# Two-layer decoder step: expert weight blocks in a ring of seven buffers, and the index-key loads moved behind the last expert's blocks

## The reference, cut to what matters

```python
y = jnp.zeros((m, d), jnp.float32)
for e in range(N_EXPERTS):
    hid = jax.nn.silu(x2 @ w_gate[e]) * (x2 @ w_up[e])
    y = y + combine[:, e:e + 1] * (hid @ w_down[e]).astype(jnp.float32)
```

```python
dots = jnp.einsum('nqhe,nke->nqhk', qi_blk, k_idx) * idx_scale
score = jnp.einsum('nqhk,nqh->nqk', jax.nn.relu(dots), wi_blk)
```

## Time and profile before

| | us |
|---|---|
| median of 3 runs (lowest, highest) | 1475.85 (1475.16, 1477.64) |
| the profiled execution: its own time | 1472.07 |
| its span | 1470.3 |
| TensorE busy in the span | 1311.3 (89%) |
| VectorE, ScalarE, GpSimd busy | 577.5, 306.4, 184.2 |
| bytes moved by DMA | 341.06 MB, mean 232 GB/s |

### The profile page before, as it was taken

One profiled execution on the slowest core, in us unless ns is written; L12 is line 12 of the kernel. 1 busy time (PEld: TensorE's weight loads), 2 busy tenths in 40 slices (PEclk: granted clock), 3 DMA queues, 4 the chain that ended last, 5 costly groups with the idle time before them and its releaser, 6 DMA issues. The chain is left out here.

```text
span 1470.3 us, 27309 instructions
## 1 busy us (share of the span) xinstructions
PE 1311.3 (89%) x10905; PEld 734.8 (50%) x10906; DVE 577.5 (39%) x1433; ACT 306.4 (21%) x785; POOL 184.2 (13%) x469
## 2 busy tenths in 40 slices
PE   7999999999599999886799998889995999998990
PEld 3444455544365556553644444555543655555550
DVE  2059944443523111011648995565216131111115
ACT  2121144421100000001313115555402000000002
POOL 1010082010100000002102661000101000000002
PEclk9999999999699999998799998999997899999995
DMA  9451489934587999999201133331514589999966
GB/s 283 166 157 59 147 289 324 347 130 129 183 332 277 394 394 399 404 413 357 63 1 58 33 115 116 115 116 59 229 72 172 198 322 360 394 387 400 406 273 204
DMA packets 87597, 341.06 MB, mean 232 GB/s; under 512 B 25843, under 2 KB 33107, under 8 KB 73506
## 3 DMA queue, kind: packets, MB, share of 16 engines
q1 hardware_dynamic: 67466, 289.49, 52.5%
q0 software_dynamic: 10656, 37.56, 7.4%
q10 hardware_dynamic: 9344, 12.20, 2.4%
HBM read 309.09 MB, written 30.47 MB: 231 GB/s over the span
## 5 line engine op out<-in xcount | busy, mean ns | idle before, releaser
L1255 PE MATMUL banks<-arena 128*32 128x128 f32 (+1 forms) x4736 | 355.0, 332 | 26.9 <-DMA arena<-in_wstream 13.0
L1255 PEld LDWEIGHTS banks<-arena 128*32 128x32 f32 (+1 forms) x4736 | 237.5, 125 | 143.9 <-issue 47.4
L1283 PE MATMUL banks<-arena 128*64 128x512 f32 (+1 forms) x1184 | 173.0, 492 | 1.1 <-ACT arena L1751 1.1
L930 PE MATMUL banks<-arena 128*128 128x512 f32 x320 | 143.9, 604 | 1.4 <-DMA arena<-in_wstream 1.4
L1857 DVE TENSOR_TENSOR arena<-arena,banks 128x256 f32<-128x256 f32 (+5 forms) x84 | 38.5, 459 | 269.4 <-PE banks L1255 175.9
L2228 DVE COPY arena<-banks 128x256 f32<-128x256 f32 (+1 forms) x56 | 21.4, 382 | 294.0 <-PE banks L1268 287.7
L1857 DVE TENSOR_TENSOR arena<-banks,arena 128x512 f32<-128x512 f32 (+5 forms) x159 | 70.6, 474 | 131.6 <-ACT arena L1673 86.0
L1158 PE MATMUL banks<-arena 128*128 128x512 f32 x256 | 113.9, 602 | 3.6 <-ACT arena L1791 2.3
L958 PE MATMUL banks<-arena 128*128 128x512 f32 x256 | 116.5, 600 | 0.0
L1751 ACT ACTIVATE arena<-banks 128x512 f32<-128x512 f32 (+1 forms) x56 | 29.6, 529 | 366.7 <-PE banks L1283 366.7
L1283 PEld LDWEIGHTS banks<-arena 128*64 128x64 f32 (+1 forms) x1184 | 58.6, 123 | 84.4 <-issue 70.0
(11 more groups left out here) (292 smaller groups left out, 1421.3 us busy)
## 6 DMA issues: line engine op xcount, KB each, us to landing
arena<-in_wstream SPq DMA_DIRECT2D x109, 2048.0 KB, 13.4
arena<-in_fox_kt SPq DMA_DIRECT2D x64, 256.0 KB, 4.5
arena<-in_fox_v SPq DMA_DIRECT2D x64, 256.0 KB, 4.2
arena<-in_dsa_page SPq DMA_DIRECT2D x64, 256.0 KB, 4.1
expert_rows<-arena ACTq DMA_DIRECT2D x76, 128.0 KB, 9.0
expert_rows<-arena POOLq DMA_DIRECT2D x1, 6656.0 KB, 20.3
hn_scratch<-arena POOLq DMA_DIRECT2D x8, 512.0 KB, 3.0
expert_rows<-arena ACTq DMA_DIRECT2D x68, 32.0 KB, 8.3
```

Of the source, the lines that this page charges most:

```text
L930: last = mm(bank(job % 4), xt[:, c, c0:c1], w[:, c, :], start=(c == 0), stop=(c == DC - 1))
L1255: last = mm(bank(b, 0, 4 * n, n * j, n * j + n), x[:, c, :], w[:, c, 4 * n * j:4 * n * j + 4 * n], start=(c == 0), stop=(c == DC - 1))
L1283: last = mm(bank(3, 0, 8 * n, n * q, n * q + n), ht2[g % 2][:, 128 * i + n * j:128 * i + n * j + n], w[:, c, 8 * n * q:8 * n * q + 8 * n], ...
```

## The change

The buffers of the expert weights become one ring of seven for each layer: the six of before and `QT` 0 to 4096 as the seventh. Block n of the layer (n = 3 s + i) goes into buffer n % 7 and waits for the use of block n-7. The first six blocks are loaded as before; block 6 (expert 2's gate) is the first in the seventh buffer and waits for nothing but `ranked`.

Index keys also live in `QT` 0 to 4096, so their 64 loads leave the early part of SP's list. They now stand behind all expert blocks of layer 0, after a wait until expert 13's down products are done (the last user of the seventh buffer), and ahead of the three blocks of layer 1's input projection, of `last_rows(0)` and of all that follows.

Semaphores are merged: `lf_dve` and `lf_act` become `lf`, and `ln_var`, `ln_root` and `ln_done` become `ln`, with counts that stand for the same events.

```diff
+SLOTS = 7
...
+              "weights": tuple(16 * len(range(i, 3 * NE, SLOTS)) for i in range(SLOTS)),
...
-    slots = [[[ring[2], ring[0], ring[1]], over_w], [[ring[1], ring[2], ring[0]], over_w]]
+    slots = [[ring[i] for i in first] + over_w + [at("QT", 0, 4096)] for first in ((2, 0, 1), (1, 2, 0))]
...
+    def slot_of_block(l, s, i):
+
+        return slots[l][(3 * s + i) % SLOTS]
+
+    def block_landed(l, s, i):
+
+        n = 3 * s + i
+        return f"weights{l}_{n % SLOTS}", 16 * (n // SLOTS + 1)
+
+    def block_used(l, s, i):
+
+        before, j = divmod(3 * s + i - SLOTS, 3)
+        name = ("gate_mm", "up_mm", "down_mm")[j] + str(l)
+        return name, upto(name, ENDS[before])
...
         def experts(l):
             b = first_block(l, "moe")
             if l == 0:
-                index_keys(0, 12)
-                sp.wait_ge(S("ln_done"), 1)
+                sp.wait_ge(S("ln"), 3)
                 first_weights(0, 1, 0)
-                index_keys(12, 24)
             sp.wait_ge(S(f"out_mm{l}"), upto(f"out_mm{l}", 5))
             first_weights(l, 0, 1)
-            if l == 0:
-                index_keys(24, 50)
             sp.wait_ge(S(f"out_mm{l}"), upto(f"out_mm{l}", 10))
             first_weights(l, 0, 2)
-            if l == 0:
-                index_keys(50, 58)
             sp.wait_ge(S(f"route_t{l}"), upto(f"route_t{l}", 3))
             first_weights(l, 1, 2)
-            if l == 0:
-                index_keys(58, NS * NPG)
             sp.wait_ge(S(f"ranked{l}"), upto(f"ranked{l}", 1))
             for s in range(2, NE):
                 k = sp.value_load(block_i[0:1, s:s + 1], min_val=0, max_val=3 * NE - 3)
-                for i, name in enumerate((f"gate_mm{l}", f"up_mm{l}", f"down_mm{l}")):
-                    sp.wait_ge(S(name), upto(name, ENDS[s - 2]))
+                for i in range(3):
+                    if 3 * s + i >= SLOTS:
+                        name, count = block_used(l, s, i)
+                        sp.wait_ge(S(name), count)
                     sp.wait_ge(S("x_in_0"), 16)
                     weights(l, s, i, a["wstream"][bass.ds(k + (b + i), 1)].rearrange("a p w -> (a p) w"))
...
         experts(0)
+        sp.wait_ge(S("down_mm0"), upto("down_mm0", ENDS[13]))
+        index_keys(0, NS * NPG)
         for b, name in ((1, "gate_mm0"), (2, "up_mm0"), (3, "down_mm0")):
             k = first_block(1, "in") + b
             sp.wait_ge(S(name), upto(name, ENDS[14]))
```

More of the change, by code:

```diff
@@ L120 @@
     (64, "vnew"),
-    (128, "xg weights"),
+    (128, "xg"),
 )
@@ L527, in weights @@
         def weights(l, s, i, src):
-            sp.dma_start(slots[l][s % 2][i], src).then_inc(S(f"weights{l}_{3 * (s % 2) + i}"), 16)
+            sp.dma_start(slot_of_block(l, s, i), src).then_inc(S(block_landed(l, s, i)[0]), 16)
         def first_weights(l, s, i):
@@ L1261, in landed @@
             def landed(s, i):
-                pe.wait_ge(S(f"weights{l}_{3 * (s % 2) + i}"),
-                           upto(f"weights{l}_{3 * (s % 2) + i}", 16 * (s // 2 + 1)))
+                name, count = block_landed(l, s, i)
+                pe.wait_ge(S(name), upto(name, count))
             def turn_hid(g):
@@ L1278, in down @@
                     pe.wait_ge(S(f"y_ev{l}"), upto(f"y_ev{l}", g))
-                w = g3(slots[l][s % 2][2], 4)
+                w = g3(slot_of_block(l, s, 2), 4)
                 for c in range(4):
@@ L1295, in experts @@
                     pe.wait_ge(S(f"silu{l}"), upto(f"silu{l}", g))
-                part_features(0, g3(slots[l][s % 2][0], DC), x, n).then_inc(S(f"gate_mm{l}"), 1)
+                part_features(0, g3(slot_of_block(l, s, 0), DC), x, n).then_inc(S(f"gate_mm{l}"), 1)
                 if g > 0:
@@ L1304, in experts @@
                     pe.wait_ge(S(f"ht_ev{l}"), upto(f"ht_ev{l}", g - 1))
-                part_features(1 + g % 2, g3(slots[l][s % 2][1], DC), x, n).then_inc(S(f"up_mm{l}"), 1)
+                part_features(1 + g % 2, g3(slot_of_block(l, s, 1), DC), x, n).then_inc(S(f"up_mm{l}"), 1)
                 if g == ENDS[s] - 1 and s + 1 < NE:
@@ L1384, in beside_even @@
                 if t == 0:
-                    pe.wait_ge(S("lf_dve"), 1)
+                    pe.wait_ge(S("lf"), 1)
                 pe.wait_ge(S("u_ready"), t + 1)
@@ L1617, in project_even @@
                 if job == 10:
[L1618 to L1621, removed]
+                    act.wait_ge(S("lf"), 1)
+                    af(lf_tmp[0], lf_tmp[0], ACT.Exp).then_inc(S("lf"), 1)
+                    act.wait_ge(S("lf"), 3)
+                    af(lf_tmp[0], lf_tmp[0], ACT.Ln).then_inc(S("lf"), 1)
                 if 12 <= job < 22:
@@ L1786, in _ @@
         af(tick[0], tick[0], ACT.Sqrt)
-        act.wait_ge(S("ln_var"), 1)
-        af(lnv, lnv, ACT.Sqrt).then_inc(S("ln_root"), 1)
-        act.wait_ge(S("ln_done"), 1)
+        act.wait_ge(S("ln"), 1)
+        af(lnv, lnv, ACT.Sqrt).then_inc(S("ln"), 1)
+        act.wait_ge(S("ln"), 3)
         for c in range(4):
@@ L2331, in _ @@
         v.scalar_tensor_tensor(out=lf_tmp[0], in0=lf_tmp[1], scalar=-1.0, in1=lf_tmp[1], op0=ALU.mult, op1=ALU.min)\
-            .then_inc(S("lf_dve"), 1)
+            .then_inc(S("lf"), 1)
         step(v.tensor_scalar(lf_tmp[2], lf_tmp[1], 0.0, None, ALU.min))
@@ L2343, in new_logf @@
         def new_logf():
-            dve.wait_ge(S("lf_act"), 1)
-            v.tensor_scalar(lf_tmp[0], lf_tmp[0], 1.0, None, ALU.add).then_inc(S("lf_dve"), 1)
+            dve.wait_ge(S("lf"), 2)
+            v.tensor_scalar(lf_tmp[0], lf_tmp[0], 1.0, None, ALU.add).then_inc(S("lf"), 1)
         def split_logf():
-            dve.wait_ge(S("lf_act"), 2)
+            dve.wait_ge(S("lf"), 4)
             tt(lft, x3[2], x3[0], ALU.subtract).then_inc(S("logf"), 1)
@@ L2418, in layer_norm @@
             v.tensor_scalar(lnv[:, 0:SEQ], bank(7), 1e-5, None, ALU.add)
-            v.tensor_scalar(lnv[:, SEQ:TOK], bank(6, 0, 64), 1e-5, None, ALU.add).then_inc(S("ln_var"), 1)
-            dve.wait_ge(S("ln_root"), 1)
+            v.tensor_scalar(lnv[:, SEQ:TOK], bank(6, 0, 64), 1e-5, None, ALU.add).then_inc(S("ln"), 1)
+            dve.wait_ge(S("ln"), 2)
             step(v.reciprocal(lnv, lnv))
             tt(xt[:, 0:4, 0:SEQ], conv_p, bc_mid(lnv[:, 0:SEQ], 4), ALU.mult)
-            tt(xt[:, 0:4, SEQ:TOK], conv_s, bc_mid(lnv[:, SEQ:TOK], 4), ALU.mult).then_inc(S("ln_done"), 1)
+            tt(xt[:, 0:4, SEQ:TOK], conv_s, bc_mid(lnv[:, SEQ:TOK], 4), ALU.mult).then_inc(S("ln"), 1)
         attend(0, 4, lambda t: causal[:, 384 - 128 * t:512])
```

## The result

The changed kernel takes 1504.59 us, the median of 4 runs (1502.66 to 1509.0), against 1475.51 us before (4 runs, 1475.14 to 1477.64): a ratio of 1.0198 (95% interval 1.017 to 1.0227), so +25 to +33 us, about +29. The forecast was 1502, +26.2.

What follows compares the result with a forecast made beforehand. It took block landing to bound the experts' second part and SP's chain the seam behind layer 0: +32.1 us for the later gather, -5.9 in layer 1, +26.2 on 1475.85, 1502 us; 8-in-10 range 1489 to 1513.

Steps and rivals of the forecast that it cites:

- The bound and the seventh buffer: Both layers' experts: later blocks set the pace; a seventh buffer gains one block's landing, 5.9 us in each layer.
- SP's time for the keys: Behind layer 0's last expert blocks: SP needs 47.7 us to issue 64 keys, plus 2 us if full queues hold it up.
- rival A: At the late keys: SP is held up to the far bound of 13.4 us, 11.4 us more, 1513 us; chance 0.15.
- The queue in front of the store: Behind the keys: the last rows' store waits for three projection blocks, 6.3 MB; third lands at 719.4, gather starts near 720.5.
- Rival B: Behind the keys: the rows store overtakes the blocks, gathers sharing engines cost up to 10.6 us; 1488 to 1499 us; chance 0.10.
- The sum at the seam: Between layer 0's experts and the combine: keys, hold-up and queue together start the gather 32.1 us later, near 720.5.
- Nothing takes the delay back: After layer 0's gather: all that follows is a chain from it, so the 32.1 us delay stays.
- The rule on small transfers: Key loads of 32 KB: overhead is SP's 0.7 us each; the coalescing rule speaks against placing them on the chain.
- The early part: Before and early in layer 0's experts: taking the key loads out is worth nothing, as TensorE is busy from 400 us.
- C: Expert stages: the seventh buffer gives nothing, since the engines are full anyway; +38 us, 1514 us; chance 0.05.
- D: Expert stages: the seventh buffer takes away all weight waits, 11.5 us more gained, 1487 us; chance 0.06.
- E: Behind layer 0's experts: key issue hides behind the last two experts, leaving only both gains, -11.8, 1464 us; chance 0.03.

Runs made afterwards that it cites:

- kernel 8: Against the kernel before: seven buffers, with projection blocks, rows store and tail weights first, then all 64 keys in one piece; 1469.58 us, ratio 0.9957.
- Kernel 3: Also rows_before_blocks: the changed kernel with the last rows' store between the keys and the three projection blocks; 1501.16 us, ratio 1.0158 to the kernel before.
- rows_by_act: The changed kernel with the last rows' store issued by ScalarE, whose queue is empty, instead of SP; 1484.09 us, ratio 1.0062 to the kernel before.
- kernel 6: Against the kernel before: seven buffers in both layers, the 64 keys spread over SP's rests in three pieces; 1468.28 us, ratio 0.9928; again 1466.94 us, 0.9935.
- kernel 7: The spread key order of kernel 6 with six buffers instead of seven; 1475.42 us, ratio 0.9986 to the kernel before.
- kernels 5: Against the kernel before: seventh buffer in layer 1 alone, layer 0 with six and its keys early; 1473.38 us, ratio 0.9961.

## Why the prediction was right, point by point

**The bound and the seventh buffer.** Right in kind, and in size over many profiles. I forecast one block in each layer, 5.9 us. The means of the table differ by 5.1 us in layer 0 and 6.4 us in layer 1; by time, the seventh buffer in layer 1 alone gave 5.8 us. TensorE's waits for blocks fall from a mean of 12.1 to 7.5 us in layer 0 and from 12.5 to 7.3 in layer 1; in the 15 stages with seven buffers 5 to 9 us of them stay, as they should when blocks land at the pace of the engines. The lead itself shows in layer 1: the last expert block landed 278.1 us behind the start of the stage before (issued at 1408.7, landed 13.4 us later), and 271.2 us in the changed kernel (1432.1, 25.8 us).

The first profile of the changed kernel alone would have misled: its layer 0 shows 289.03 us, a gain of 1.3, and its last block landed 275.2 us behind the start (issued at 643.1, landed 29.1 us later) against 275.3 before. In that one stage the lead was lost before the end. Its timeline of PE (start, us, what, idle before):

```profile
397.04 11.90 PE L1268 MATMUL banks<-arena 128*64 128x256 f32 x128 [1.11 <-DVE arena L1870]
...
645.34 5.31 PE L1268 MATMUL banks<-arena 128*64 128x256 f32 x32 [3.61 <-issue]
...
684.14 1.93 PE L1296 MATMUL banks<-arena 128*32 128x256 f32 x32 [0.53 <-ACT arena L1764]
```

Its first 128 products ran 11.90 us, against 10.71 in the profile before; the granted clock of the stage's first 12 us was 0.75 of full speed here and 0.85 there. The 32 products behind the wait of 3.61 us took 5.31 us in place of 3.67, with a granted clock of 0.72 over the 6 us from 645.34 on. These are means of stretches that ran in part at the lower of the two clock levels, 1.2 and not 2.4 GHz. Why the blocks landed late in that execution is not shown. The other six layer-0 stages with seven buffers lie between 284.3 and 287.1, so I take it for scatter.

**SP's time for the keys.** Forecast 47.7 us, and 2 us for a hold-up. Measured 50.0 in the changed kernel, 49.4 with six buffers, 47.7 in kernel 8. The sum 49.7 was right, in part by luck. The forecast put the hold-up down to full queues. A single issue took up to 1.54 us against a median of 0.469, but only one of the long ones (1.25 us, at 663) stands where expert blocks were still under way and keys took 4.5 us and more to land. Those of 1.54, 0.99 and 0.96 us stand at 679, 688 and 692, where keys landed in 3.4 us or less, and the row of kernel 8 has one of 1.58. So what makes them long stays open; nothing came near the 13.4 us of rival A. The forecast also passed over the slowest of the three rows of keys in the same view of the kernel before:

```profile
292.91 9.34 SPq L547 DMA_DIRECT2D arena<-in_kidx_t  x12
```

That is 0.78 us each, which makes 49.8 us for 64 without any second term.

**The queue in front of the store.** Forecast: 19.8 us from the first block's issue to the gather, 18.7 of them until the third block is down. Measured: 708.80 to 728.42, 19.6 us, with the third block down at 726.9, 18.1 us behind the first issue. Kernel 3 shows the cause: with the store ahead of the blocks, 3.0 us. The order on each ring that the Trainium skill states ("DMA: Bandwidth & Descriptors", queues, rings and completion order) agrees with this trace: the stores landed at about 727.0 us, behind the third block's 726.9. Its warning that completion is not first in, first out across a queue didn't show in this place. Rival B was also priced too low: the gathers then share the engines with the blocks, as said, but this costs 14.8 us and not up to 10.6.

**The sum at the seam.** Forecast: gather 41.8 us behind the experts' end (720.5 less 678.7). Measured: 42.4 and 42.7, and 42.0 with six buffers. The delay of the gather, forecast as 32.1 us, was 40.0 in the first profile and 37.3 in the second. In the first it stood at 728.42 and not 720.5: 2.8 us of that is the late start of the stage, 4.5 its small gain in layer 0, 0.6 the seam. In the second it stood at 725.75: 2.9 us are the late start, 1.4 what the gain in layer 0 fell short, 0.9 the seam. So the seam was right to 1 us, and what is left over is what differs from one execution to the next; the close total (+26.2 against +29 and +26) rests on medians in which that evens out.

**Nothing takes the delay back.** Right. From the gather to layer 1's first expert product it is 458.3 and 457.6 us in the two profiles of the changed kernel, 455.6 before, and in seven others 455.4 to 460.0. The two left are rows_by_act (473.7, with its added wait of 17.1 us) and rows_before_blocks (470.9, with its slow gathers).

**The rule on small transfers** (the Trainium skill, "DMA: Bandwidth & Descriptors", rules for kernel authors: coalesce, under 64 KB one pays mostly overhead). The keys' price was SP's 0.78 us each on the chain. But kernels 6 and 8 keep all 64 small loads, and kernel 6 loses nothing by them, kernel 8 some 3 to 4 us: here the place decided. What fewer and larger loads would have cost in the old place no run shows.

**The early part.** Costed at nothing, and kernel 7 agrees: with the keys gone from there, six buffers are no faster than before within its interval (-4.9 to +0.7 us). The start of layer 0's experts says the same: 394.2 us by the mean of the three profiles with all or half of the keys early, 394.9 by that of the nine without.

**The rivals.** A fell with the keys' row, B with kernel 3, C with kernels 5 and 7 (the same order with and without the seventh buffer: -10.7 and -2.1 us), D with the 5 to 9 us of waits that stay. E was held impossible in this order, and was: it takes another order, that of kernel 6, in which SP's time is spread between waits. There the forecast of -11.8 us for two bare gains is met by -10.7 and -9.6.

**Two slips.** The DMA digit is 9 in slices 13 to 18 and 33 to 37 of the earlier trace rows, where the forecast says 13 to 17 and 32 to 38; and 698.5 + 2 makes 700.5, not 700.7. Nothing else hangs on either.

## What to carry to other kernels

Loads that cost nothing in bytes can cost their issuer's time: count the issues by the nearest row of that queue, and ask what stands behind them in the same list. Where a stage runs at the pace of a transfer that never rests, one more buffer was worth about one block's landing time, once, and not the sum of the waits. To free one held-up instruction shows only who is late next; put the short stores and the first-needed loads ahead, and let the cheap many go out while somebody else has work.

## What the runs showed of the hardware

Two things I had not expected. The length of an expert stage with the same code and the same buffers differs by 3 to 5 us between profiles: layer 0 with seven buffers took 289.0 and 285.9 us in two executions of the changed kernel, and 284.3 to 289.0 over all seven profiles. That is nearly the gain looked for; one profile can't show it, the mean of several did. And gathers that share the engines with three blocks of 2 MB slow down by about as much as the blocks take: 30.0 us from the gather's start to TensorE's return against 15.2, with 6.3 MB more to move, which at the 398 GB/s of the earlier trace rows are 15.8 us.
